# The order of statements on four engines between the first z projection and slot 47 of a hybrid decoder layer

## What is computed

```
h = x
h = h + concat(attn_out, ssd_out) @ w_out            # inputs: rms_norm(h) @ w_in
#   attn_out: 8 heads, window 128, softmax with sinks and bias
#   ssd_out : rms_norm(ssd_scan(...) * silu(z))      # z is one slice of rms_norm(h) @ w_in
xn = rms_norm(h)
q  = (xn @ w_query)                                  # 8 heads x 2 halves x 128
s1, s2 = q1 @ sub_keys1.T, q2 @ sub_keys2.T          # 128 scores each
v1, i1 = top_k(s1, 16);  v2, i2 = top_k(s2, 16)
top_s, pos = top_k(v1[:, None] + v2[None, :], 16)    # 16 experts of 256 candidates
idx = i1 * 128 + i2 at pos;  gates = softmax(top_s)
u   = expert_down[idx]                               # per token: 8 heads x 16 experts
act = gelu(u . xn) * gates
h   = h + sum(act * expert_up[idx])
out = rms_norm(h)
```

## Time and profile before

| | us |
|---|---|
| median of three runs | 1528.83 (1527.42 to 1529.14) |
| the profiled execution's own time | 1526.34 |
| its span, first to last instruction | 1524.5 |
| PE busy in the span | 1325.1 (87%) |
| POOL busy | 1108.3 (73%) |
| DVE busy | 1053.0 (69%) |
| ACT busy | 441.6 (29%) |

### The profile page before, as it was taken

One profiled execution on the slowest core, in us unless ns is written; L12 is line 12 of the kernel. 1 busy time (PEld: TensorE's weight loads), 2 busy tenths in 40 slices (PEclk: granted clock), 3 DMA queues, 4 the chain that ended last, 5 costly groups with the idle time before them and its releaser, 6 DMA issues.

```text
span 1524.5 us, 14446 instructions
## 1 busy us (share of the span) xinstructions
PE 1325.1 (87%) x4392; PEld 678.5 (45%) x4392; DVE 1053.0 (69%) x2534; ACT 441.6 (29%) x1216; POOL 1108.3 (73%) x1005
## 2 busy tenths in 40 slices
PE   8999998899888998889889898889888878888886
PEld 5557974444444443444444443434444334434432
DVE  3546598886776777677766676777777676667664
ACT  2123462122323232233223222233233222222222
POOL 0001134548899898888999998888999888888893
PEclk9999999999999999999999999999999999999999
DMA  7640069999999999999999999999999999999995
GB/s 254 172 184 12 1 259 413 412 418 422 421 420 422 421 421 422 421 421 421 421 421 418 421 416 422 422 421 409 408 421 423 420 422 422 421 421 421 416 415 231
DMA packets 85217, 569.80 MB, mean 374 GB/s; under 512 B 10227, under 2 KB 12564, under 8 KB 18708
## 3 DMA queue, kind: packets, MB, share of 16 engines
q0 software_dynamic: 73728, 536.90, 85.1%
q1 hardware_dynamic: 11412, 31.99, 6.2%
HBM read 565.19 MB, written 3.67 MB: 373 GB/s over the span
## 4 chain that ended last, share of the span: by engine, by line
DMA 32%; PE 30%; POOL 21%; DVE 10%; issue 4%; ACT 3%; SPq 0%; DVEq 0%; ACTq 0%; POOLq 0%
DMA arena<-in_experts_du_dram,arena 27%; PE ps L1477 14%; POOL arena L419 11%; POOL arena L409 8%; PE ps L1245 5%; DMA wide<-in_experts_du_dram,arena 5%; PE ps L1416 3%; DVE arena L1053 3%; PE ps L1451 3%; POOL wide L409 2%; ACT arena L647 1%; DVE wide L1053 1%; ACT arena L468 1%; PE ps L1260 1%; PE ps L1232 1%
## 5 line engine op out<-in xcount | busy, mean ns | idle before, releaser
L1477 PE MATMUL ps<-arena 128*128 128x512 f32 x1624 | 774.7, 621 | 141.6 <-ACT arena L647 133.0
L409 POOL DMA_INDIRECT arena<-in_experts_du_dram,arena x418 | 488.0, 1168 | 120.1 <-issue 63.8
L1477 PEld LDWEIGHTS ps<-arena 128*128 128x128 f32 x1624 | 307.3, 196 | 565.7 <-issue 329.9
L419 POOL TENSOR_SCALAR arena<-ident,arena 128x128 f32<-128x128 f32 x464 | 494.8, 1066 | 47.5 <-PE ps L1477 31.9
L1053 DVE CUSTOM_DVE_ANT_0 arena<-arena,wide 128x1024 f32<-128x1024 f32 x210 | 255.3, 1229 | 138.3 <-DMA arena<-in_experts_du_dram,arena 137.5
L1053 DVE CUSTOM_DVE_ANT_0 arena<-arena 128x1024 f32<-128x1024 f32 x208 | 252.6, 1228 | 114.8 <-DMA arena<-in_experts_du_dram,arena 114.1
L643 ACT ACTIVATE arena<-arena 128x2 f32<-128x2 f32 (+1 forms) x234 | 47.5, 203 | 762.0 <-DVE arena L1053 761.7
L1477 PE MATMUL ps<-wide,arena 128*128 128x512 f32 x376 | 183.2, 610 | 29.8 <-ACT arena L647 26.1
L647 ACT ACTIVATE arena<-arena 128x128 f32<-128x128 f32 x464 | 161.1, 394 | 8.1 <-ACT arena L643 0.2
L409 POOL DMA_INDIRECT wide<-in_experts_du_dram,arena x94 | 107.5, 1144 | 60.9 <-DVE arena L1037 24.0
L1477 PEld LDWEIGHTS ps<-wide,arena 128*128 128x128 f32 x376 | 70.0, 194 | 124.8 <-issue 73.6
(11 more groups left out here) (197 smaller groups left out, 1028.4 us busy)
## 6 DMA issues: line engine op xcount, KB each, us to landing
arena<-in_w_in_blocks_dram SPq DMA_DIRECT2D x16, 512.0 KB, 9.5
arena<-in_experts_du_dram,arena POOLq DMA_INDIRECT x418, 16.4
wide<-in_w_query_dram SPq DMA_DIRECT2D x5, 1024.0 KB, 9.3
wide<-in_w_out_dram SPq DMA_DIRECT2D x1, 4096.0 KB, 17.8
h<-in_x_dram SPq DMA_DIRECT2D x4, 512.0 KB, 9.7
arena<-in_w_query_dram SPq DMA_DIRECT2D x2, 1024.0 KB, 6.4
arena<-in_x_t_dram SPq DMA_DIRECT2D x3, 512.0 KB, 6.5
line_scratch<-arena SPq DMA_DIRECT2D x1, 1536.0 KB
```

The costliest lines, as they stand in the source:

```text
L409: gp.indirect_dma_start(rows[b], None, experts_du, bass.IndirectOffsetOnAxis(ap=idx[:, (q // PH) % 2, q % PH * TOPK + i:q % PH * TOPK + i ...
L419: g.tensor_scalar(diag(s), ident[:], eg[:, q % 2, i:i + 1], None, ALU.mult).then_inc(sem("gate_diag"), 1)
L1477: last = mm(acc(t, b)[:], diag(s), up[:, b * 512:(b + 1) * 512], start=(s % SLOTS == 0), stop=False, skip_group_check=True)
```

## The change

Only the order of statements changes, and the place of six rows. No operation is added or taken away, and every wait inside a statement stays, save that the gathers' waits follow their rows to new numbers (row 3 is now the query/key memory, row 4 the SSD input memory, rows 5 and 7 the bias and the probabilities, row 6 the SSD output), and that `dots` and `experts` of the first 48 slots are written in pairs where they were in fours. The gates stay in fours.

The core of the diff (PE's list from slot 16 on goes on in the same way, pairs of experts and pairs of pieces in turn):

```diff
-        rows = [slot(14, 2, wide), slot(4, 2), slot(6, 2), slot(9, 2), slot(12, 2, wide), slot(0, 2, arena2),
-                slot(2, 2, arena2), slot(20, 2), slot(22, 2), slot(11, 2), slot(15, 2)]
+        rows = [slot(14, 2, wide), slot(4, 2), slot(6, 2), slot(20, 2),
+                slot(9, 2), slot(0, 2, arena2), slot(12, 2, wide), slot(2, 2, arena2),
+                slot(22, 2), slot(11, 2), slot(15, 2)]
...
                 elif s == 3:
+                    gp.wait_ge(sem("score_ps"), 2 * NT)
+                elif s == 4:
                     gp.wait_ge(sem("y_ps"), NT)
                     gp.wait_ge(sem("off_read"), NT - 1)
-                elif s == 4:
-                    gp.wait_ge(sem("mixS_ready"), NT)
                 elif s == 5:
                     gp.wait_ge(sem("score_sb"), 4 * NT)
                 elif s == 6:
-                    gp.wait_ge(sem("pv_ps"), NT)
-                elif s == 7:
-                    gp.wait_ge(sem("score_ps"), 2 * NT)
-                elif s == 8:
+                    gp.wait_ge(sem("mixS_ready"), NT)
+                elif s in (7, 8):
                     gp.wait_ge(sem("pv_ps"), NT)
...
# POOL
+            skip(3)
             gather(0)
-            skip(3)
+            gather(1)
             gather(2)
+            gather(3)
             add_off(3)
-            gather(3)
+            gather(4)
+            gather(5)
             gate(3)
+            gather(6)
             gather(7)
-            gather(1)
-            gather(5)
-            gather(4)
             gather(8)
-            gather(6)
+            gather(9)
             gather(10)
-            gather(9)
             gather(11)
...
# ACT
+            gates_z(2)
+            query(1)
+            squared_y(2)
             softmax(2, 0)
+            mixed(1, 1)
             softmax(2, 1)
-            squared_y(2)
-            mixed(1, 1)
+            exp_gates(0)
             turned(2, 0)
...
-            squared_y(3)
             mixed(2, 1)
             softmax(3, 0)
+            squared_y(3)
             turned(3, 0)
...
# DVE
+            ssd_norm(1)
             attended(1)
-            go(v.tensor_copy(iota16, iota16i[:]))
-            ssd_norm(1)
+            search_halves(0)
             scores(2, 0)
             ssd_inputs(3)
-            ssd_masks(3)
+            search_sums(0)
+            z_product(2)
             scores(2, 1)
             maxima(2)
-            search_halves(0)
-            search_sums(0)
             search_indices(0)
+            ssd_masks(3)
             ssd_norm(2)
             attended(2)
             z_product(3)
+            scores(3, 0)
             ssd_state(3)
-            scores(3, 0)
-            ssd_diagonal(3)
             scores(3, 1)
             maxima(3)
+            ssd_diagonal(3)
             dots(0, 1)
...
-            dots(8, 4)
+            dots(8, 2)
+            dots(10, 2)
             gates(8, 4)
-            dots(12, 4)
-            search_halves(2)
+            dots(12, 2)
+            dots(14, 2)
             gates(12, 4)
...
# PE
             turn_probs(2, 0)
             turn_probs(2, 1)
-            query(1)
+            keyed(1)
             turn_probs(2, 2)
             turn_mix(1, 0)
             turn_probs(2, 3)
             attend(2)
             ssd_off(3)
             scores(3, 0)
-            ssd_diagonal(3)
-            scores(3, 1)
             turn_mix(2, 1)
-            keyed(1)
+            pieces(0, 1)
+            scores(3, 1)
+            pieces(1, 2)
+            ssd_diagonal(3)
             query(2)
             turn_probs(3, 0)
+            pieces(2, 4)
             turn_probs(3, 1)
-            pieces(0, 1)
+            turn_mix(2, 0)
             turn_probs(3, 2)
-            pieces(1, 2)
-            turn_mix(2, 0)
             turn_probs(3, 3)
             attend(3)
+            pieces(4, 6)
             turn_mix(3, 1)
             experts(0, 1)
+            turn_mix(3, 0)
+            experts(1, 1)
+            experts(2, 2)
+            experts(4, 2)
+            experts(6, 2)
+            pieces(6, 8)
+            experts(8, 2)
             keyed(2)
-            experts(1, 1)
-            turn_mix(3, 0)
-            experts(2, 2)
-            pieces(2, 4)
-            pieces(4, 8)
-            experts(4, 4)
+            experts(10, 2)
+            experts(12, 2)
+            experts(14, 2)
+            pieces(8, 10)
+            pieces(10, 12)
             query(3)
```

More of the change, by code:

```diff
@@ L449, in _ @@
             gather(14)
+            gather(15)
             gather(16)
-            gather(15)
             gather(17)
@@ L1155, in _ @@
             gates(0, 1)
+            attended(3)
             dots(1, 1)
[L1157 removed]
             gates(1, 1)
```

178 lines of the change are left out of this document (99 added, 79 removed).

## The result

| | median | lowest to highest | runs | profiled execution (span) |
|---|---|---|---|---|
| before | 1527.22 | 1525.72 to 1530.36 | 20 | 1526.34 (1524.5) |
| after | 1532.63 | 1526.85 to 1538.18 | 20 | 1533.05 (1531.3) |

The ratio is 1.0036, with a 95% interval of 1.0026 to 1.0045: the change costs some 5.4 us. The forecast took -1.4 from a median of three runs, 1528.83; against the 20 runs here the same -1.4 would be 1525.8, so the difference was missed by 6.8. Two of the change's 20 runs (1526.85 and 1527.03) are where the forecast was; the others reach up to 11 above it. Why those two were fast is not known, since neither was profiled.

The account below looks back on a forecast made before the run. The eighth gather, released by the end of attend(3), was taken to set the end. Terms -0.3 (attend(3) start), +0.1 (tenth gather) and -1.2 (break at 264) sum to -1.4: 1528.83 to 1527.4 us, range 1522.5 to 1531.5.

Parts of the forecast that it names:

- What bounds the kernel: Stream of gathers: the eighth, released by the end of attend(3), sets the program's end, not the first.
- the rival of the first gather: Start of the stream: 6 us earlier first gather comes through, 1521.6, or half of it, 1524; chance 0.20.
- First gather, attend(2), scores, maxima(3): Ahead of tile 3's softmax: gather 0 6 us earlier without effect; maxima(3) ends 1.15 earlier in all.
- VectorE beside the gathers, "nothing": Tail of tile 3: gathers sharing DVE's port could cost up to 3 x 1.6 us; nothing was added.
- Softmax of tile 3: ACT's square between the two softmax halves costs 0.82, without a wait for gate(3); attend(3) starts 0.3 earlier.
- "As before" for attend(3) itself: From the softmax to the third transpose that releases attend(3), work is as before; no term for attend(3)'s duration.
- The tenth gather: Right behind attend(3): issue near 229.7, needed near 229.9; cost 0 to 1, taken as 0.1.
- The break at 264: Stream at 264 to 272 us: the 23rd gather goes out near 257, the break closes, worth 1.2 us.
- both places that the text named: Possible new breaks at gathers 26 (near 271, needed 273) and 32 (near 288, needed 290); cost nothing.
- the cover of "2 us each": Gathers 26 and 32: each issued 2 us before it is needed, so neither costs anything.
- Pairs, "nothing": dots and experts written in twos: PE work same in sum, DMA stream the cover after slot 47; no effect.
- Query weights late: Rival: weights landing at 217 hold query(2) on PE, shifting everything from attend(3) on by 5, 1532.4; chance 0.12.

Follow-up runs that it names:

- e3: Changed kernel with gather 0 held until the first half of tile 3's scores is done: 1536.35 us.
- e1: Changed kernel with pieces(2, 4) and pieces(4, 6) put between the transposes of tile 3 on PE: 1529.89 us, ratio 1.0015 to before.
- e2: Changed kernel with three filler products added in PE's two waits between tile 3's transposes, nothing moved: 1529.06 us, ratio 1.0016 to before.
- e4: Kernel before with its two pieces moved from between tile 3's transposes to behind attend(3): 1530.54 us, ratio 1.0021 to before.
- e10: e5 with DVE's search_indices(2) and add_projection(1, 1) also placed as in the kernel before: 1529.71 us, ratio 1.0021 to before.
- e11: e10 without the filler products at tile 3's transposes: 1532.85 us, ratio 1.0044 to before.
- e5: e2 with PE's order of slots 12 to 23 set back towards that of the kernel before: 1531.80 us.
- e6: Changed kernel with PE's order behind slot 11 as in e5, without the filler products: 1537.42 us.
- e15: e2 with one filler product more in each of PE's two waits between attend(0) and turn_mix(0, 0): 1527.28 us, ratio 1.0003 to before.
- e17: Changed kernel with e15's two early filler products alone, none at tile 3's transposes: 1532.54 us.
- e16: e15 with three more filler products ahead of the experts of slot 12: 1526.96 us, ratio 0.9999 to before.
- e14: Kernel before with four filler products ahead of the experts of slot 12 and three ahead of those of slot 20: 1525.39 us, ratio 0.9987.
- e8: Kernel before with nine filler products in PE's wait ahead of the experts of slot 12: 1528.25 us, ratio 1.0012.
- e12: e10 with four more filler products ahead of the experts of slot 16: 1532.42 us, ratio 1.0039 to before.

## Why the prediction was wrong, point by point

- **What bounds the kernel**: right as far as it went. The eighth gather is paid, the first is not paid one for one (e3: 11.0 for 3.7), and 6.3 of an earlier first gather brought no gain: the rival of the first gather falls. Whether those 6.3 did nothing at all is not shown, since e3 puts the first gather behind its old place.
- **First gather, attend(2), scores, maxima(3)**: starts near 194, 199.9, 204.5 and 209.8 were forecast; 193.87, 198.87, 203.50 and 208.96 came. From `attend(2)` on the count was 0.8 to 1.0 too late.
- **VectorE beside the gathers, "nothing"**: right. maxima(3) took 2.29 again, with gathers at 207.67, 210.94 and 212.20 around it, and none of DVE's one-column operations on the tail took more than 0.22.
- **Softmax of tile 3**: ACT's square (215.07) between the halves, as forecast, behind a wait of 0.60 where none was forecast. The profile puts that wait down to ACT itself, but POOL's `gate(3)` (L377), now behind six gathers, ran from 213.16 to 214.99, as forecast, while the first softmax half was done early. The start of `attend(3)` came at 220.51 (forecast 220.8): close in part by luck, because the count ahead of maxima(3) was 0.8 too late and this wait was left out.
- **"As before" for attend(3) itself: this is the step that failed.** The sum has a term for the start of `attend(3)` (-0.3) and none for its duration, which was put at no change without a reason: the text took it, and those of the pieces and the `turn_mix` behind it, from rows at full clock, 3.79, and wrote of the pieces that they "end near 217, before ACT needs them" as if it were a good thing. It was the loss: they had been the cover. The duration was 7.09, so that `attend(3)` ended 2.7 later than before where 0.3 earlier was forecast. That it costs is shown by e1, e2, e4 and the pairs e10 and e11, e5 and e6, e15 and e17, which differ in fillers alone; its price is 2.7 to 5.6 by version.
- **The tenth gather**: 0 to 1 was allowed; it came 6.5 behind the eighth, 1.5 more than the two transfers of 2.49 that it had. The reason is the same: PE L1411 stood behind `attend(3)` and `pieces(4, 6)` at half clock. In e2 it goes out at 227.96, 4.9 behind the eighth and in time.
- **The break at 264**: the 23rd gather was forecast near 257 and came at 263.26, in e2 at 257.59. Behind the eighth gather that is 32 forecast and 35.4 and 34.5 measured, where 38 was needed: the old break did close. But a new one came at both places that the text named. The gathers of slots 26 and 32 were forecast 46 and 63 behind the eighth, with 48 and 65 needed; in e2, at full clock in `attend(3)`, they came 49.4 and 65.8 behind it, in the changed kernel 50.3 and 66.7. So the cover of "2 us each" was not there even without the fall at tile 3, though e2 still has half clock at 235 to 240 and 255 to 260. e2 has 392 GB/s from 264 to 300, below before's 403, so the -1.2 of the sum is near +0.9 on that trace.
- **Pairs, "nothing"**: not tested alone; the loss at 330 to 360 (2.5 by the rates) lies behind the reordered slots 36 to 47, in what was called covered.
- **Query weights late**: refuted; `query(2)` ran at 210.01 without a wait.
- Of the 5.4, then: taken from the changed kernel itself, 2.7 to 3.6 come back with the fall at tile 3; about 2 are left, seen in the traces as the breaks at 264 to 300 and 330 to 360 and as an early fall in some executions. e15 and e16 are level with before, but no single edit was shown to carry this part, and its cause stays open. Nor do they bring back the forecast gain: fillers made the old order faster as well (e14, 1.9).

## What to carry to other kernels

Work that stands between two waits on TensorE may be its cover: when an order is changed, look at how busy the engine is just ahead of each long run of products on the path, before and after, and not only at when the operands are ready. A duration taken from a trace holds at the clock it was measured at. A filler of products that nobody reads is a cheap test of this. It has to end before the wait does (e8 lost 1.3), and even then it may gain nothing (e17; e12 was slower than e10).

## What the runs showed of the hardware

- TensorE's clock can fall without a long idle stretch: behind waits of 0.91 and 1.57 us amid transposes (PE busy for 1.51 of 4 us) the granted clock went to 0.50, that is 1.2 GHz, at 220.5 and stayed there until about 230.7, though PE had no gap from 219.97 to 231.
- The clock can also fall in one execution and not in another, of the same instructions: e10 and e12 are the same program up to 259, and from 135.5 to 138 one has 1.00 and the other 0.50.
- The loss at one break can't be read as the loss of the kernel: e17, with the late tenth gather of the changed kernel, has 418 GB/s from 264 to 300 where the changed kernel has 390, and 371 from 330 to 360 where that has 387, and both medians are within 0.1 of each other. Why the breaks moved is not known.
